# Where the modulation weights are multiplied: VectorE with a partition sum instead of TensorE products, behind the first eight blocks

## The reference, cut to what matters

```python
silu_c, silu_cc = jax.nn.silu(c), jax.nn.silu(c_ctx)
for i in range(DEPTH):                                     # DEPTH = 2
    m  = (silu_c  @ w_mod[i] + b_mod[i]).reshape(bsz, N_MOD, 1, D_MODEL)   # N_MOD = 9, D_MODEL = 1024
    mc = (silu_cc @ w_mod[i] + b_mod[i]).reshape(N_MOD, D_MODEL)
    h = _ffn_half(h, norm_g[i, 0], m[:, 0], m[:, 1], m[:, 2], ffn_w_in[i, 0], ffn_w_out[i, 0])
    ...
    h = _ffn_half(h, norm_g[i, 2], m[:, 6], m[:, 7], m[:, 8], ffn_w_in[i, 1], ffn_w_out[i, 1])
```

## Time and profile before

| what | value |
| --- | --- |
| median of three runs | 4673.69 us (4672.83 to 4674.70) |
| span of the profiled execution | 4671.1 us |
| TensorE busy | 4428.6 us (95%), 24682 products |
| VectorE busy | 1640.5 us (35%) |
| ScalarE busy | 1816.1 us (39%) |
| GpSimd busy | 2644.5 us (57%) |
| chain that ended last, TensorE's share | 86% |
| modulation products (L408) | 640 records, 21.6 to 822.0 us |
| mean granted TensorE clock | 0.972 |

### The profile page before, as it was taken

One profiled execution on the slowest core, in us unless ns is written; L12 is line 12 of the kernel. 1 busy time (PEld: TensorE's weight loads), 2 busy tenths in 40 slices (PEclk: granted clock), 3 DMA queues, 4 the chain that ended last, 5 costly groups with the idle time before them and its releaser, 6 DMA issues.

```text
span 4671.1 us, 62602 instructions
## 1 busy us (share of the span) xinstructions
PE 4428.6 (95%) x24682; PEld 3748.6 (80%) x24682; DVE 1640.5 (35%) x3161; ACT 1816.1 (39%) x2941; POOL 2644.5 (57%) x1282
## 2 busy tenths in 40 slices
PE   8999999999999989889989999999898999999998
PEld 5777777778778889876888888887877888888886
DVE  2211222022012332364568522223454668322223
ACT  3222322232233343443232555554442333555554
POOL 3433244334444377641166888888630367888886
PEclk8999999999999999999999999999999999999999
DMA  6622366222232244440143255555440242455554
GB/s 259 241 102 95 68 243 243 90 82 99 90 108 90 74 153 172 175 155 28 46 145 131 100 189 189 189 187 204 167 145 19 77 145 91 146 187 188 189 189 158
DMA packets 100139, 659.22 MB, mean 141 GB/s; under 512 B 10464, under 2 KB 16864, under 8 KB 22368
## 3 DMA queue, kind: packets, MB, share of 16 engines
q1 hardware_dynamic: 90000, 638.46, 37.5%
q10 hardware_dynamic: 9936, 17.86, 1.5%
HBM read 646.84 MB, written 9.44 MB: 140 GB/s over the span
## 4 chain that ended last, share of the span: by engine, by line
PE 86%; DVE 7%; ACT 3%; POOL 2%; issue 1%; DMA 1%; SPq 0%; ACTq 0%; DVEq 0%; POOLq 0%
PE ps L2911 14%; PE ps L253 14%; PE ps L254 13%; PE ps L255 13%; PE ps L2901 8%; PE ps L2902 4%; PE ps L2821 3%; PE ps L2617 3%; PE ps L1503 2%; POOL ring_rest L269 2%; PE ps L408 1%; PE ps L1673 1%; DVE arena L2339 1%; PE ps L1642 1%; PE ps L2007 1%
## 5 line engine op out<-in xcount | busy, mean ns | idle before, releaser
L269 POOL TENSOR_TENSOR ring_rest<-ring,rounded 128x1024 fp32r<-128x1024 f32 x960 | 2350.0, 2462 | 1462.6 <-ACT rounded L241 1261.7
L253 PE MATMUL ps<-part,rounded 128*128 128x256 f32 (+1 forms) x3456 | 1188.2, 344 | 81.4 <-DVE part L2447 22.4
L254 PE MATMUL ps<-part,rounded 128*128 128x256 f32 (+1 forms) x3456 | 1176.0, 340 | 0.0
L255 PE MATMUL ps<-part,ring_rest 128*128 128x256 f32 (+1 forms) x3456 | 1174.2, 340 | 0.0
L253 PEld LDWEIGHTS ps<-part,rounded 128*128 128x128 f32 x3456 | 670.1, 194 | 183.7 <-issue 26.8
L241 ACT ACTIVATE rounded<-ring 128x1024 fp32r<-128x1024 f32 x496 | 496.5, 1050 | 698.8 <-PE ps L255 689.3
L255 PEld LDWEIGHTS ps<-part,ring_rest 128*128 128x128 f32 x3456 | 669.4, 194 | 69.1
L254 PEld LDWEIGHTS ps<-part,rounded 128*128 128x128 f32 x3456 | 670.4, 194 | 67.2
L3000 ACT ACTIVATE rounded<-ring 128x1024 fp32r<-128x1024 f32 x464 | 490.2, 1056 | 332.2 <-DMA ring<-in_weights 330.0
L2901 PE MATMUL ps<-x_parts,rounded 128*128 128x512 f32 x1728 | 616.8, 397 | 1.5 <-ACTq L2835 1.5
L2911 PE MATMUL ps<-rounded,part 128*128 128x512 f32 x2048 | 593.4, 394 | 16.8 <-POOL ring_rest L269 10.1
(11 more groups left out here) (362 smaller groups left out, 5357.5 us busy)
## 6 DMA issues: line engine op xcount, KB each, us to landing
ring<-in_weights SPq DMA_DIRECT2D x528, 1024.0 KB, 4.8
arena<-in_mod_weights SPq DMA_DIRECT2D x72, 1024.0 KB, 7.9
held<-arena ACTq DMA_DIRECT2D x20, 256.0 KB, 5.6
arena<-held SPq DMA_DIRECT2D x20, 256.0 KB, 4.5
arena<-bias_scratch ACTq DMA_DIRECT2D x2, 2048.0 KB, 12.8
bias_scratch<-arena ACTq DMA_DIRECT2D x1, 3072.0 KB, 32.1
x<-in_x SPq DMA_DIRECT2D x1, 2048.0 KB, 9.5
arena<-in_keys ACTq DMA_DIRECT2D x2, 1024.0 KB, 4.9
```

The lines of the kernel that those rows point to most:

```text
L253: mm(out, w[0], a[0], start=start, stop=False)
L254: mm(out, w[0], a[1], start=False, stop=False)
L255: return mm(out, w[1], a[0], start=False, stop=stop)
L269: eng.tensor_tensor(c.ring_rest[:, slot, half], c.ring[:, slot, half], c.rounded[:, (self.s0 + r) % ROUNDED, half].bitcast(F32), ALU.subtr ...
```

## The change

The first eight blocks stay as they are in work, only laid out anew (two vectors, one k, 1 MB). Everything behind them is recut:

- The weights come in chunks of 0.5 MB: one vector (1024 columns) by one k. A *unit* is what fills two accumulators of 128 x 1024 (`acc`, in SBUF): one vector for both streams, or, for the vectors 5 to 8 of layer 1, of which only the token stream is wanted, two vectors for one stream. Each layer has seven units of 16 VectorE operations: `tensor_scalar` for k = 0 (two a unit), `scalar_tensor_tensor` (chunk x condition + accumulator, the condition one number a partition) for the other 14. Units of both streams read 8 chunks, each used twice, the two last ones of layer 1 read 16, each used once.
- The units are spread over *turns*, one a block: three turns for each of the first six units, two for the last (turns 18 and 19). Of a three-turn unit of 8 chunks the turns hold 6, 6 and 4 operations, of one of 16 chunks 6, 5 and 5, and a last unit's hold 8 and 8. `weigh(dve, j)` is VectorE's last work in round j.
- `sum`: once the last operation of a unit is done, TensorE sums each accumulator over the partitions with a 128 x 32 block of ones, four products of 512 columns, behind block j where the unit closed in turn j - 1. `keep_rows` follows on ScalarE in the same round, `turn` behind the next block, `add` in VectorE's next round, before `weigh`.
- The ring has four chunk buffers. SyncE's queue waits for the weighing of chunk c - 4 before it issues chunk c, behind the load of a ring block.
- The accumulators lie where `cst1` was. The table is no longer loaded at the start; its two parts are loaded by ScalarE's queue in the `Project` stages behind the two sides.
- `Project` no longer waits for the side at its start but before its third tile (m = 6, `side_banks`).

```diff
-MOD_BLOCKS = 36
 MOD_LEAD = 8
-MOD_RING = 2
+MOD_RING = 4
...
+A_ACC = A_CST1
...
+    LENGTHS = (3,) * 6 + (2,)
...
+        first = 2 if lead else 0
+        both = N_MOD if layer < DEPTH - 1 else 5
+        self.units = [[(j, 0), (j, 1)] for j in range(first, both)]
+        self.units += [[(j, 0), (j + 1, 0)] for j in range(both, N_MOD, 2)]
+        assert len(self.units) == len(self.LENGTHS)
+        self.starts = [sum(self.LENGTHS[:u]) for u in range(len(self.units) + 1)]
+        self.chunks = [(u, j, k) for u, parts in enumerate(self.units) for k in range(KD)
+                       for j in sorted({j for j, s in parts})]
+        self.turn_of, self.ops = {}, 0
+        self.taken = []
+        for c, (u, j, k) in enumerate(self.chunks):
+            mine = [i for i, x in enumerate(self.chunks) if x[0] == u]
+            self.turn_of[c] = self.starts[u] + (c - mine[0]) * self.LENGTHS[u] // len(mine)
+            self.taken.append(self.ops)
+            self.ops += sum(i == j for i, s in self.units[u])
...
+    def load(self, sp, c):
+        slot, _ = self.loads(c)
+        if c >= MOD_RING:
+            sp.wait_ge(self.weighed.sem, self.weighed.at(self.taken[c - MOD_RING + 1]))
+        elif self.lead:
+            sp.wait_ge(self.summed.sem, self.summed.at(1))
+        else:
+            sp.wait_ge(self.weighed.sem, self.weighed.at(0))
+        u, j, k = self.chunks[c]
+        sp.dma_start(self.chunk_buffer(c), self.chip.io["mod_weights"][self.layer, j, k]).then_inc(self.chip.mod_loaded[slot], 16)
...
+    def loads_after(self, turn):
+        return [c for c in range(MOD_RING, len(self.chunks)) if self.turn_of[c - MOD_RING] == turn]
+    def weigh(self, dve, turn):
+        v = self.nc.vector
+        for c, (u, j, k) in enumerate(self.chunks):
+            if self.turn_of[c] != turn:
+                continue
+            slot, count = self.loads(c)
+            dve.wait_ge(self.chip.mod_loaded[slot], count)
+            op = self.taken[c]
+            for a, (i, s) in enumerate(self.units[u]):
+                if i != j:
+                    continue
+                w, weight = self.chunk_buffer(c), self.cond[:, k, s:s + 1]
+                if k == 0:
+                    if u:
+                        dve.wait_ge(self.summed.sem, self.summed.at(u + self.earlier))
+                    last = v.tensor_scalar(self.acc[:, a], w, weight, None, ALU.mult)
+                else:
+                    dve.wait_ge(self.weighed.sem, self.weighed.at(op - 1))
+                    last = v.scalar_tensor_tensor(self.acc[:, a], w, weight, self.acc[:, a], ALU.mult, ALU.add)
+                last.then_inc(self.weighed.sem, 1)
+                op += 1
+    def closed_in(self, turn):
+        return [u for u in range(len(self.units)) if self.starts[u + 1] - 1 == turn]
+    def sum(self, pe, u):
+        c = self.chip
+        end = max(i for i, x in enumerate(self.chunks) if x[0] == u)
+        pe.wait_ge(self.weighed.sem, self.weighed.at(self.taken[end + 1]))
+        if u + self.earlier:
+            pe.wait_ge(self.rows_kept.sem, self.rows_kept.at(u + self.earlier))
+        for g in range(self.SETS):
+            a, h = divmod(g, 2)
+            last = self.nc.tensor.matmul(c.ps[g * self.TILE:(g + 1) * self.TILE, self.BANK, :], c.ones[:, 0:self.TILE],
+                                         self.acc[:, a, h * 512:(h + 1) * 512], start=True, stop=True)
+        last.then_inc(self.summed.sem, 1)
...
-            k = steps * (i - 8 * n) + e
...
-                at = (e * self.SETS + g) * width
-                last = mm(c.ps[g * self.TILE:(g + 1) * self.TILE, self.BANK + n % 2, 0:width], self.cond[:, k, :],
-                          w[:, at:at + width], start=k == 0, stop=k == KD - 1)
-        last.then_inc(c.mod_done, 1)
...
+    def lead_products(self, pe):
...
     def keep_rows(self, act, n):
...
+        self.nc.scalar.activation(self.rows, self.chip.ps[:, self.BANK, :], ACT.Copy).then_inc(self.rows_kept.sem, 1)
...
+            parts = self.units[n - self.earlier]
+            turned = c.ps[:, self.TURNED, 0:32].rearrange("p (m a h s) -> p a h m s", a=2, h=2, s=2)
+            for a, (j, s) in enumerate(parts):
+                m = self.mods[:, j, :, s].rearrange("p (h m) -> p h m", m=4)
+                b = bias[:, KD * j:KD * (j + 1)].rearrange("p (h m) -> p h m", m=4)
+                last = v.tensor_tensor(m, turned[:, a, :, :, 0], b, ALU.add)
+            link(last)
+            done = sorted({j for j, s in parts})
+            streams = 2 // len(done)
+        for j in done:
+            self.finish(link, j, streams)
...
     def released(self, pe):
+        pass
+    def side_banks(self, pe):
...
-                for n in self.side.closed_after(j - 1):
-                    self.side.turn(pe, n)
-                for i in self.side.blocks_after(j):
-                    self.side.block(pe, i)
+                for u in self.side.closed_in(j - 2):
+                    self.side.turn(pe, u + self.side.earlier)
+                for u in self.side.closed_in(j - 1):
+                    self.side.sum(pe, u)
...
-                for n in self.side.closed_after(j):
-                    self.side.keep_rows(act, n)
+                for u in self.side.closed_in(j - 1):
+                    self.side.keep_rows(act, u + self.side.earlier)
...
-                for n in self.side.closed_after(j - 1):
-                    self.side.add(dve, link, n)
+                for u in self.side.closed_in(j - 2):
+                    self.side.add(dve, link, u + self.side.earlier)
+                self.side.weigh(dve, j)
...
+                    if self.hidden and first and m == 6:
+                        self.hidden.side_banks(pe)
...
+    def load_table(self, act):
+        side, (first, end) = self.table
+        act.wait_ge(side.summed.sem, side.summed.at(len(side.units) + side.earlier))
+        act.dma_start(self.chip.at(A_CST1, NCST1)[:, first:end], self.chip.io["cst1"][:, first:end]).then_inc(self.chip.cst1_loaded, 16)
...
-            sp.dma_start(chip.at(A_CST1, NCST1), io["cst1"]).then_inc(chip.cst1_loaded, 16)
+            for i in range(MOD_RING):
+                chip.sides[0].load(sp, i)
             plan = {}
             for stage in stages:
                 if isinstance(stage, FeedForwardIn) and stage.side:
+                    if not stage.side.lead:
+                        plan[stage.b0] = [(stage.side, i) for i in range(MOD_RING)]
                     for j in range(KF):
-                        plan[stage.b0 + j] = [(stage.side, i) for i in stage.side.blocks_after(j)]
+                        plan[stage.b0 + j + 1] = [(stage.side, i) for i in stage.side.loads_after(j)]
```

153 lines of the change are left out of this document (74 added, 79 removed).

## The result

| | median of the runs | profiled span | ratio to before, 95% interval |
|---|---|---|---|
| before | 4673.3 us (4 runs beside these) | 4671.1 us | |
| after | 4695.6 us (4694.9 to 4700.8) | 4693.8 us | 1.005 (1.0036 to 1.0065) |

The change costs 22 us of the median and 22.7 us of the span; forecast were +30.9 us, with 4676 to 4726 as the range. The direction, the mechanism and most of its places came as predicted, at three quarters of the size.

A forecast was written before the change was run, and what follows sets the result against it. TensorE was taken to set the pace. Input stages cost 49.5 us instead of 32.45 (+17.1) and 53.1 instead of 41.70 (+11.4), Project +2.4: +30.9 on 4673.7 gives 4704.6 us, range 4676 to 4726.

The forecast's parts named there:

- sums and turns on TensorE: Inside each stage's rounds: seven sums at 1.2 us and six turns at 0.8 us, 13.2 us a stage.
- first unit with clock: Start of each stage: 2.65 us before block 3, 12.8 before the first sum, 3.35 for low clock and slow sum.
- middle units: TensorE waits 1.8 us before each middle sum: five in the first stage (9.0 us), four in the second (7.2).
- last unit with clock: Before each stage's last sum: 5.2 us wait in the first, 7.0 in the second, plus 3.35 for clock and slow sum.
- wait for m = 6: Second Project: three linked operations each wait for a GpSimd half, so TensorE loses 2.4 us (bounds 0 and 4.7); first hidden.
- the wait before block 3: First unit: VectorE's L710 of round 1 queues behind turn 0, so TensorE starts block 3 2.65 us late.
- The clock at the sums: First and last sums: after TensorE's idle, low clock costs 2.35 us and the slow sum 1 us more, 3.35 together.
- The rule on `S2S2D2_STT`: Skill page: VectorE's form with two non-bf16 SBUF sources halves throughput; the forecast rejected it, taking 1.29 us for 1024 columns.
- Hidden: Rival: VectorE gets through without waiting for GpSimd and every sum finds its unit done; 4626 us, chance 0.11.
- Only start and end: Rival: tighter middle turns remove the 16.2 us of middle waits, and end clock losses and port term shrink; 4684, chance 0.12.
- Spacing of 1.3 us: Rival: wider spacing of VectorE's operations makes middle waits 2.6 instead of 1.8 us for nine units; 4717, chance 0.15.
- half rate: Rival: VectorE's weighing takes 2.2 us for 1024 columns, some 13 us more for each of 13 units; about 4880, chance 0.03.

The follow-up runs named there:

- the one with 8 columns: The changed kernel with the accumulating weighing operations (k over 0) on 8 of 1024 columns, sums, turns and loads kept; 4636.6 us, ratio 0.9929.
- The second input's experiment: The changed kernel with each weighing operation's second tensor read from a PSUM bank instead of the SBUF accumulator; 4653.0 us, ratio 0.9959.

## Why the prediction was right, and by how much not

The rows "measured" are differences of the windows by unit between the kernel after and the one with 8 columns; the last unit of the second stage is held against that of the first (23.94 us), since its own has the loads in it.

| step | forecast, stages 1 / 2 | measured |
|---|---|---|
| sums and turns on TensorE | 13.2 / 13.2 | 14.3 / 14.3 |
| first unit with clock | 18.8 / 18.8 | 17.8 / 17.6 |
| middle units | 9.0 / 7.2, and 3.6 for turn 17 | 6.7 / 7.6 |
| last unit with clock | 8.55 / 10.35 | 7.5 / 10.2 |
| wait for m = 6 | 0 / 2.4 | 0 / 0 |
| behind the second stage | 0 | 1.1 |

*Right.* Strict turns between GpSimd and VectorE carried the first unit's walk to 0.1 us of its end (107.0 against 107.1; its turn 0 ends at 82.64 against 82.65) and the wait before block 3 to a few hundredths (2.86 us from start to start, less the usual 0.23, for 2.65). That the sum's wait is 10.96 us and not 12.8 isn't another walk: the clock fell for some products behind the wait at block 3 already, block 3 ended 1.65 us later, and TensorE had that much less to wait. The second input's experiment shows the cause of the first unit's and most of the middle waits, the later ones what the place is worth; the last units have another cause (below). That the short middle waits leave the clock alone came true (1.00).

*The clock at the sums*, counted twice. The prediction took 2.35 us for 4.7 us at the low level and 1.0 more for the slow sum, but the sum lies inside those microseconds. From 107.07 to 112.10 the granted clock is 0.50, sum and all, which costs 2.5 us for 3.35; at the last unit of the first stage it is 0.50 from 319.66 to 323.70, 2.0 us. That the last unit's row comes near (7.5 for 8.55) hides a wait of 5.5 us for 5.2.

*TensorE's work*, 1.1 us short: a turn costs 0.95 us in a round (11.83 against 10.88), not 0.8. In the kernel before it stood beside modulation blocks and cost 0.76 (13.76 against 13.00), so the restart of the large products, which I counted for a sum, seems to follow a turn too when it stands alone.

*The middle units*, 5.5 us too much of 19.8. The operations start 1.19 to 1.2 us apart, as taken, and in a unit like the walk's the last four end at T + 24.1 for 24.3; less the longer turn that leaves 1.57 us for 1.8 (1.77 in another unit). But the walk had `add` with a factor before the weighing everywhere. Where the unit before has no factor, as at 162.98, the first operation already waits when GpSimd's second half ends, the sixth ends 0.45 us sooner behind its block (T + 13.9 for 14.4), GpSimd's pair is held up for 5.53 us and not 5.98, and the wait is 1.1 us:

```profile
128.73 7.26 DVE L430 SCALAR_TENSOR_TENSOR arena<-arena 128x1024 f32<-128x1024 f32 x6 [0.23 <-DVE mods L490]
...
162.98 8.95 DVE L430 SCALAR_TENSOR_TENSOR arena<-arena 128x1024 f32<-128x1024 f32 x6 [0.23 <-DVE mods L509]
```

The unit that closes in turn 17 of the second stage costs 2.1 us for 3.6.

*The last unit of the second stage* came out at 10.2 for 10.35 by luck. The step adds 1.8 us of loads to 5.2 us of VectorE and 3.35 of clock; measured are a wait of 8.6 us for 7.0 and 1.5 for the clock, and without VectorE's work 9.1 of the 10.2 us stay. So the loads set this unit, not VectorE. VectorE's rows in the kernel after show it:

```profile
846.97 1.28 DVE L430 SCALAR_TENSOR_TENSOR arena<-arena 128x1024 f32<-128x1024 f32 x1 [0.84 <-DMA arena<-in_mod_weights]
848.79 1.28 DVE L430 SCALAR_TENSOR_TENSOR arena<-arena 128x1024 f32<-128x1024 f32 x1 [0.54 <-DMA arena<-in_mod_weights]
```

A chunk is issued only when one four before it is used, and lands 4.1 us later in the median. The prediction counted this chain alone. But the DMA engines have no slack there either: in the kernel with 8 columns the last four chunks are issued by 785.84 and land 1.28 us apart, with the DMA engines busy throughout (in the kernel after their share is 0.95 from 846.50 to 853.00):

```profile
786.50:793.00 6.50, 0.16 (x1) 0.00 (x0) 0.92 (x5) 0.60 (x1) 0.00 (x0) 0.92 1.03 422
```

No run separates the chain from the bytes.

*The wait for m = 6* failed in one assumption: that each of the three linked operations has to wait for a half. The kernel after has

```profile
869.62 0.17 DVE L487 TENSOR_SCALAR mods<-mods 128x8 f32<-128x8 f32 x1
869.83 2.28 DVE L488 TENSOR_TENSOR mods<-mods,vec 128x8 f32<-128x8 f32 x1
872.14 2.30 DVE L490 TENSOR_SCALAR mods<-mods 128x8 f32<-128x8 f32 x1
...
869.73 9.37 POOL L268 TENSOR_TENSOR ring_rest<-ring,rounded 128x1024 fp32r<-128x1024 f32 x4 [29.40 <-ACT rounded L240]
```

The first one started 0.11 us before GpSimd and slipped through, so two halves were waited for and the last was over at 874.4, 0.4 us before TensorE came to m = 6. Where the turn lies one block later, the first had to wait as well, and TensorE lost 2.0 us before m = 6. So the mechanism holds, but whether it cost 0 or 2 us hung on a tenth of a microsecond.

*The rule on `S2S2D2_STT`.* A weighing takes 1.28 us where nothing disturbs it, with both inputs in SBUF, and 1.27 us with one of them in PSUM. The Trainium skill's "Vector Engine (DVE) Microarchitecture Reference", section "Points that are easy to get wrong", has the first form at half throughput; the trace disagrees at this size too. Of the shared port, the Trainium skill's "SBUF — State Buffer", section "Who interferes with whom", has the right mechanism: the edit that takes the second SBUF input away takes the alternation with it. Its lock for a whole instruction is more than the rows give: an operation of 1.28 us lengthens GpSimd's pair from 4.76 to 5.7 to 6.0 us, so by 0.95 to 1.2.

*The rivals.* "Hidden" is 70 us away at 4626, and even without VectorE's load the kernel has 4637, mostly since the loads of the last unit remain. "Only start and end" had 4684. The start and the end are 53 of the 67 us of waits and lost clock, but the forecast had that too (56.5 of 76.3); the middle waits, which this rival put at nothing, are 14.3 us for the forecast's 19.8. The measured 4695.6 lies 11.6 us from this rival and 9.0 from the forecast. Spacing of 1.3 us and half rate are out by the rows.

*Still open.* Why the clock comes back later behind the norm after the second stage (the 1.06 us of the span) isn't explained, nor what holds up the k = 0 operation with its one tensor input. Nor is it tried what the first sum costs when GpSimd's four halves at the start are spread over more rounds.

## What to carry to other kernels

An engine that is 35% busy can take over work only where it has its slack. Write down for each operation that is moved what else uses its port and its queue at that moment, and walk the first and the last unit, for they are unlike the middle: here 53 of 67 us of waiting and lost clock came from four units of fourteen.

Once such a move has lost, don't ask first whether it is too much work, but shift it: one turn later, another cut over the turns and another order of units turned +22 us into -27 us with the same operations. The one turn alone gave 33 of these 49 us; the single steps behind it are hardly clear of the runs' noise.

## What the runs showed of the hardware

- Under a backlog on both sides, VectorE and GpSimd alternate strictly, and what VectorE waits doesn't depend on its own size: an operation on 8 columns in the Project rows takes 2.28 us, a whole GpSimd half. With one of its two inputs in PSUM no operation of 196 took over 1.282 us; with both in SBUF the longest took 3.421.
- TensorE's clock after a stop, in two windows of the kernel after: behind 2.86 us between two products' starts (80.43 to 83.30) the granted clock is, from 1.9 us after the restart, for 3 us at 0.50, its level of 1.2 GHz; behind 1.87 us (143.92 to 145.79) it stays at 1.00, 2.4 GHz.

```profile
85.20:88.20 3.00, 3.00 (x9) 2.32 (x8) 3.00 (x2) 1.08 (x2) 2.78 (x2) 0.50 0.99 401
143.90:150.00 6.10, 4.62 (x24) 2.81 (x23) 5.05 (x5) 3.50 (x5) 4.03 (x2) 1.00 0.80 255
```

- The place of one input is worth as much here as half the columns: 4653.0 us with a PSUM input, 4656.5 us with 512 columns.
